# Expert weights of a mixture-of-experts stage: fifteen places for raw slabs and five for their high parts, in place of five and three

## The reference

```python
def grouped_moe(x, w_router, router_bias, w_gate, w_up, w_down):   # 512 tokens, 16 experts in 4 groups of 4
    scores = jax.nn.sigmoid(t @ w_router)
    ...
    g_idx = jnp.argmax(group_score, axis=-1)             # one group of 4 experts for each token
    _, e_local = lax.top_k(in_group, TOP_K)              # 2 of these 4
    ...
    h = silu(einsum('td,edf->tef', t, w_gate)) * einsum('td,edf->tef', t, w_up)   # d 1024, f 256
    y = einsum('tef,efd->td', h * combine[..., None], w_down)
```

## Time and profile before

| | |
|---|---|
| median of 3 runs | 3222.83 us |
| the profiled execution, its own time | 3222.16 us |
| its span, first to last instruction | 3220.1 us |
| granted TensorE clock, mean of the span (1 is 2.4 GHz) | 0.935 |
| PE busy | 2928.7 us (91%) |
| DVE, ACT, POOL busy | 1568.6, 1215.3, 826.5 us |
| slabs of 512 KB: SP, issue to landing, median | 3.7 us (202 transfers) |
| chain that ended last, share of PE | 74% |

### The profile page before, as it was taken

One profiled execution on the slowest core, in us unless ns is written; L12 is line 12 of the kernel. 1 busy time (PEld: TensorE's weight loads), 2 busy tenths in 40 slices (PEclk: granted clock), 3 DMA queues, 4 the chain that ended last, 5 costly groups with the idle time before them and its releaser, 6 DMA issues.

```text
span 3220.1 us, 54157 instructions
## 1 busy us (share of the span) xinstructions
PE 2928.7 (91%) x22694; PEld 2317.3 (72%) x22694; DVE 1568.6 (49%) x2880; ACT 1215.3 (38%) x2134; POOL 826.5 (26%) x814
## 2 busy tenths in 40 slices
PE   7899999999889999999899899998978887898998
PEld 6788888888767878887577677777756655556566
DVE  3544555455424344342443454566667766542433
ACT  2333333333322243232433344543255655442341
POOL 4222222222122100000345243541000055523243
PEclk9899899989889999999899898999999999878999
DMA  3111111111033333332122122224327877411112
GB/s 130 37 32 41 32 41 35 41 31 38 28 111 109 102 99 96 94 97 77 43 65 70 47 69 63 82 66 151 98 81 257 275 248 230 148 38 53 36 56 69
DMA packets 101266, 283.09 MB, mean 88 GB/s; under 512 B 11392, under 2 KB 11392, under 8 KB 99744
## 3 DMA queue, kind: packets, MB, share of 16 engines
q1 hardware_dynamic: 81968, 209.11, 21.5%
q0 software_dynamic: 14592, 60.56, 5.6%
q10 hardware_dynamic: 4464, 9.96, 0.8%
HBM read 261.24 MB, written 18.35 MB: 87 GB/s over the span
## 4 chain that ended last, share of the span: by engine, by line
PE 74%; DVE 10%; ACT 8%; DMA 5%; issue 2%; POOL 1%; ACTq 0%; DVEq 0%; SPq 0%; POOLq 0%
PE psum L478 72%; DVE arena L410 5%; ACT arena L395 4%; DMA ring<-in_w 3%; ACT arena L403 3%; DMA ring<-in_w,arena_whole 2%; PE psum L482 2%; DVE arena L419 2%; DVE ring L410 2%; ACT L390 1%; POOL ring L3488 1%; DVE arena L414 1%; DVE arena L422 1%; DVE arena L434 0%; DMA arena<-in_x 0%
## 5 line engine op out<-in xcount | busy, mean ns | idle before, releaser
L478 PE MATMUL psum<-arena,ring 128*128 128x512 f32 (+3 forms) x6152 | 1442.6, 365 | 13.5 <-DVE arena L410 6.9
L478 PEld LDWEIGHTS psum<-arena,ring 128*128 128x128 f32 (+2 forms) x6152 | 1024.4, 193 | 209.0 <-issue 35.6
L478 PE MATMUL psum<-arena 32*32 32x32 f32 (+16 forms) x12460 | 880.4, 254 | 154.2 <-DVE arena L410 58.4
L478 PE MATMUL psum<-arena,arena 128*128 128x512 f32 (+1 forms) x2896 | 887.4, 391 | 93.3 <-DVE ring L410 68.1
L478 PEld LDWEIGHTS psum<-arena 32*32 32x32 f32 (+10 forms) x12460 | 626.0, 142 | 360.9 <-issue 147.0
L478 PEld LDWEIGHTS psum<-arena,arena 128*128 128x128 f32 x2896 | 525.4, 190 | 257.5 <-DVE ring L410 108.5
L422 POOL CAST ring<-ring 128x512 fp32r<-128x512 f32 x332 | 231.3, 697 | 1370.9 <-DMA ring<-in_w 1248.5
L403 ACT ACTIVATE arena<-psum 128x512 f32<-128x512 f32 (+16 forms) x676 | 290.8, 448 | 746.9 <-PE psum L478 572.5
L410 DVE TENSOR_TENSOR ring<-ring,arena 128x1024 fp32r<-128x1024 f32 (+1 forms) x298 | 352.6, 1183 | 310.5 <-ACT arena L403 305.9
L403 ACT ACTIVATE arena<-ring 128x1024 fp32r<-128x1024 f32 (+1 forms) x298 | 305.6, 1026 | 500.2 <-PE psum L478 334.5
L410 POOL TENSOR_TENSOR ring<-ring,ring 128x512 fp32r<-128x512 f32 x332 | 440.2, 1326 | 26.7
(11 more groups left out here) (50 smaller groups left out, 862.2 us busy)
## 6 DMA issues: line engine op xcount, KB each, us to landing
ring<-in_w SPq DMA_DIRECT2D x202, 512.0 KB, 3.7
ring<-in_w SPq DMA_DIRECT2D x356, 256.0 KB, 2.7
bg<-arena ACTq DMA_DIRECT2D x24, 256.0 KB, 2.3
yd<-arena ACTq DMA_DIRECT2D x7, 512.0 KB, 6.4
arena<-bg POOLq DMA_DIRECT2D x1, 3072.0 KB, 17.0
arena<-in_x SPq DMA_DIRECT2D x1, 2112.0 KB, 15.0
od<-arena POOLq DMA_DIRECT2D x8, 256.0 KB, 2.4
oy<-arena POOLq DMA_DIRECT2D x8, 256.0 KB, 3.0
```

Source lines behind the costliest of these rows:

```text
L478: self.last_ins = self.eng.matmul(out, l, r, start=start, stop=stop, skip_group_check=skip)
```

## The change

During the expert loop, ten more places take raw slabs. Four of them (`soon`) lie in memory that is free once `branches` has ended. Six (`late`) lie where the tokens `x` and two parts of `m.O` are, free once PE has transposed the tokens (event `x_trl`, 1, 3). So slab i of the stage goes to place i modulo 15 of fifteen. Places 0 to 4 of these are the ring's. The high parts get five places in place of three. The room comes from `m.xs` and `m.hot`, which now hold one pair: the selection matrices of the next pair are made in the first expert of blocks 1, 3 and 5, after their last reader, no longer a pair ahead.

```diff
+def slot_of(K, n):
+    first = K.book.now.get(("slab", "slab", "experts", 0))
+    if first is not None and first <= n < first + len(K.m2.we.offs):
+        i = (n - first) % len(K.raw)
+        return (first + i) % RING if i < RING else i
+    return n % RING
+
+def emptied_by(K, slabs):
+    last, out = {}, []
+    for n in range(len(slabs)):
+        out.append(last.get(slot_of(K, n)))
+        last[slot_of(K, n)] = n
+    return out
...
-    m.xt, m.xs, m.hot, m.ysb = M(8 * T), M(16 * T), M(4 * T), [M(1024) for _ in range(2)]
+    m.xt, m.xs, free, m.hot, m.ysb = M(8 * T), M(8 * T), [M(SLAB) for _ in range(5)], M(2 * T), [M(1024) for _ in range(2)]
...
-    wh = [M(1024), M(1024), m.O[:, 10 * T:12 * T]]
+    wh = [M(1024), M(1024), m.O[:, 10 * T:12 * T]] + free[:2]
...
+    m.soon = free[2:] + [M(SLAB)]
+    m.late = [x[:, SLAB * i:SLAB * i + SLAB] for i in range(4)] + [m.O[:, 2 * T:4 * T], m.O[:, 6 * T:8 * T]]
...
     dve_slots(K, m, pos)
     hot(0)
     dve_shares(K, m)
-    hot(1)
     for b in range(BLOCKS):
...
             if e == 0:
                 V.apart().wait_ge(*at("e_rowed", b))
                 V.apart().cp(m.sw[b % 2], out_of(K, 1, 4, "e_rows", b), "e_rows", b)
+                if b % 2 and b // 2 + 1 < PAIRS:
+                    hot(b // 2 + 1)
...
-            if g + 1 < PAIRS:
-                hot(g + 1)
...
-            slot = n % RING
-            G.wait_ge(*at(*K.P.slabs[n - RING][2]))
-            G.ready().indirect_dma_start(K.ring[:, slot * SLAB:slot * SLAB + SLAB], None, by_row,
+            slot = slot_of(K, n)
+            G.wait_ge(*at(*K.P.slabs[before[n]][2]))
+            G.ready().indirect_dma_start(K.raw[slot], None, by_row,
...
-                if n >= RING and off is not None:
-                    sp.wait_ge(*book.at(*slabs[n - RING][2]))
...
+                slot = slot_of(K, n)
+                if before[n] is not None:
+                    sp.wait_ge(*book.at(*slabs[before[n]][2]))
+                elif slot >= RING + len(m2.soon):
+                    sp.wait_ge(*book.at("x_trl", 1, 3))
+                elif slot >= RING:
+                    for e in ("pe", "act", "dve"):
+                        sp.wait_ge(*book.at("end", e, "branches"))
```

More of the change, by code:

```diff
@@ L579, in raw_of @@
     size = run.offs[i][1]
-    return n, K.ring[:, n % RING * SLAB:n % RING * SLAB + size], K.ring_r[n % RING][:, 0:size]
+    return n, K.raw[slot_of(K, n)][:, 0:size], K.ring_r[slot_of(K, n)][:, 0:size]
 def act_hi(K, run, i):
@@ L2095, in memory2 @@
     m.esg = [m.O[:, 8 * T + 256 * i:8 * T + 256 * i + 256] for i in range(4)]
-    wh = [M(1024), M(1024), m.O[:, 10 * T:12 * T]]
+    wh = [M(1024), M(1024), m.O[:, 10 * T:12 * T]] + free[:2]
     m.x_r, m.xh_r = M.rounded(x, T), M.rounded(m.xh, T)
-    m.we = Run(K, "experts", run_of(w0 + 89 * SLAB, 96) + [(None, SLAB)] * 72, wh, [("b_sum", 23)] * 3)
+    m.we = Run(K, "experts", run_of(w0 + 89 * SLAB, 96) + [(None, SLAB)] * 72, wh, [("b_sum", 23)] * 5)
     m.wrh, m.wrl = M.rounded(M(256), 128)
@@ L3175, in rows @@
             for j in range(4):
-                P.mm(bk(o)[:, 0:4], m.hot_r[4 * (b // 2 % 2) + j][:, S], w[:, 4 * j:4 * j + 4], n == 0 and j == 0, n == 1 and j == 3)
+                P.mm(bk(o)[:, 0:4], m.hot_r[j][:, S], w[:, 4 * j:4 * j + 4], n == 0 and j == 0, n == 1 and j == 3)
         P.did("e_rowed", b)
@@ L3181, in weights @@
         P.wait_ge(*at("lo", "experts", i))
-        return m.we.hi[i % 3], K.ring_r[n % RING]
+        return m.we.hi[i % len(m.we.hi)], K.ring_r[slot_of(K, n)]
     def up(b, e):
@@ L3268, in placed @@
             A.wait_ge(*at("e_xsum", g, k))
-            A.copy(m.xs_r[8 * (g % 2) + k][:], out_of(K, 1, T, "e_xs", g, k), "e_xs", g, k)
+            A.copy(m.xs_r[k][:], out_of(K, 1, T, "e_xs", g, k), "e_xs", g, k)
     def turned(b, e):
@@ L3326, in hot @@
         for j in range(4):
-            V.ts(m.hot_r[4 * (g % 2) + j][:], m.slots["number"], pos[:, j:j + 1], -256.0 * g, SUB, EQ, *(("e_hot", g) if j == 3 else ()))
+            V.ts(m.hot_r[j][:], m.slots["number"], pos[:, j:j + 1], -256.0 * g, SUB, EQ, *(("e_hot", g) if j == 3 else ()))
     def gated(b, e):
@@ L3483, in pool_experts @@
     by_row = wall.rearrange("p (s c) -> (p s) c", c=SLAB)
+    before = emptied_by(K, K.P.slabs)
     for n, (off, size, done) in enumerate(K.P.slabs):
         if off is None:
-            slot = n % RING
-            G.wait_ge(*at(*K.P.slabs[n - RING][2]))
-            G.ready().indirect_dma_start(K.ring[:, slot * SLAB:slot * SLAB + SLAB], None, by_row,
+            slot = slot_of(K, n)
+            G.wait_ge(*at(*K.P.slabs[before[n]][2]))
+            G.ready().indirect_dma_start(K.raw[slot], None, by_row,
                                      bass.IndirectOffsetOnAxis(ap=m.place[:, 4 + (done[2] - 96) // 24:5 + (done[2] - 96) // 24], axis=0),
@@ L4169, in layout_engines @@
     half = K.mem.rounded(ring[:, :], HALF)
+    K.raw = [ring[:, n * SLAB:n * SLAB + SLAB] for n in range(RING)]
     K.halves = [half[2 * n:2 * n + 2] for n in range(RING)]
@@ L4190, in layout_engines @@
     m2.floor = m1.floor
+    K.m2 = m2
+    K.raw += m2.soon + m2.late
+    K.ring_r += [K.mem.rounded(q, SLAB)[0] for q in m2.soon + m2.late]
     K.mem.limit += at["con"]["sel16"][0] - early
@@ L4271, in _ @@
             slabs = K.P.slabs
+            before = emptied_by(K, slabs)
             for n, (off, size, done) in enumerate(slabs):
-                if n >= RING and off is not None:
-                    sp.wait_ge(*book.at(*slabs[n - RING][2]))
                 if off is None:
                     continue
-                slot = n % RING
-                eng.dma_start(ring[:, slot * SLAB:slot * SLAB + size], wall[:, off:off + size]).then_inc(*book.up("slot%d" % slot, ("slot%d" % slot, n), by=16))
+                slot = slot_of(K, n)
[6 more added lines that the diff above has]
+                        sp.wait_ge(*book.at("end", e, "branches"))
+                eng.dma_start(K.raw[slot][:, 0:size], wall[:, off:off + size]).then_inc(*book.up("slot%d" % slot, ("slot%d" % slot, n), by=16))
                 if slabs[n][2] == ("slab", "gates", 27):
```

10 lines of the change are left out of this document (5 added, 5 removed).

## The result

The changed kernel takes 3149.72 us (median of 4 runs, 3143.29 to 3159.00) against 3225.18 us before (4 runs beside them, 3220.64 to 3229.49). The ratio is 0.9768, with a 95% interval of 0.9739 to 0.9798: by the ratio 74.8 us less (65 to 84). The forecast was 3140 us, 82.5 less. The profiled execution is the slowest of the four (3159.0 us), so I compare stages inside the traces, not its whole time.

What follows compares the result with a forecast made beforehand. The prediction took the five-place ring as the bound, 1.82 us a slab, with PE next. The loop falls from 356.5 to 268 + 6 = 274 us, 82.5 less: 3222.2 - 82.5 = 3139.7, said as 3140, range 3129 to 3160.

Steps and rivals of the forecast that it cites:

- The ring's turn: Expert loop: load, copy, subtraction and matmuls of one place take 9.1 us for five slabs, 1.82 us a slab.
- 268 + 6 = 274: Expert loop: PE's work sums to 268 us, plus 6 us of waits, for 274 us in place of 356.5.
- The 6 us for waits: Expert loop: added to PE's sum for low parts, DVE at 95% beside PE, and short DMA gaps; ends 1 and 20.
- the last block's debt: Last block of the loop: four more adds stand in DVE's queue (5 us); as the only loss, 1 us.
- the small work of PE: Expert loop: eight transposes and eight narrow matmuls a block, taken at 1.7 us a block, 12 us in all.
- 322 GB/s: Expert loop: DMA rate expected from the stage's own shares; 86.5 MB would take 269 us, ending at 2662, PE at 2663.
- Rival 2: Expert loop: landings get longer with more in flight; at 300 GB/s the whole takes 3153 us; chance 10%.
- Rival 1: Blocks 4 to 6: POOL's gathers set the pace from 1.97 us each; at 2.3 the whole takes 3163 us; chance 8%.
- Rival 3: Expert loop: DMA gives only 241 GB/s, the loop keeps its length, squares cost 3.1 us: whole 3226 us; chance 2%.
- Rival 4: Expert loop: DVE's low parts wait for whole gathers, 68 us more on DVE: whole 3190 us; chance 2%.
- with five it is four slabs, 5.5 us: Expert loop: with five high parts, a low part is asked for four slabs ahead of PE, 5.5 us, against 2.8 with three.
- The layer norm: Ahead of the loop: two more ACT copies delay the squares 3.1 us, covered by DVE's centring: cost 0, uncovered 3.1.

Runs made afterwards that it cites:

- the experiment: Changed kernel with DVE's four additions of the last block moved from its four experts into its last four down slabs: loop 272.3 us, whole 3157.02 us, ratio 0.9776.

## Why the prediction was right

**What bounds.** Right. The ring's turn was the bound: ten more places take away all waits for landings, and with the two high parts the loop is 80.0 us shorter where 82.5 were forecast. Four more places would have done nearly as much (278.6 us).

**The sum of the loop.** Forecast 268 + 6 = 274, measured 276.5. PE's slabs and `placed` are 232.7 + 23.1 = 255.8, and PE's waits 5.9. That leaves 14.8 us for transposes, narrow matmuls and steps between, 2.1 a block where I took 1.7. The 6 us for waits was nearly exact, but where they fall was only half foreseen: 3.5 us are the last block's debt (2.5 of it in two waits), and 2.4 are spread over the experts before. I gave that debt 1 us; the experiment gave back 4.2. So the small work of PE was put 2.8 us too low, and the split of the 6 us was wrong while its sum was right, which is luck.

**The DMA.** My 322 GB/s as the most the stage would get was too low: it ran at 364 to 367 for 40 us at a stretch. The mean over the loop is 304 GB/s, because PE asks for no more. At 365 GB/s the 86.5 MB need 237 us, so PE, with 268, is the bound by 31 us and not by a hair. The bound was rightly named, for a reason that was worse than it is. The landings in the loop did get longer, harmlessly: SP's took 5.3 and 5.5 us in the median (ring and new places), where they took 4.6 in the loop before; the 3.7 in the table of the kernel before is over the whole program. Three signs for the profile after were missed: a DMA share above 0.9 (0.83 over the loop), over 310 GB/s (304), and landings above 6 us, which only 49 of POOL's have (6.3). All three hang on the DMA being nearly the bound, which it was not. Rival 2 is out.

**Rival 1** is out by 25.5 us, and was the right one to watch. **Rival 3** is out with 276.5 us. **Rival 4** is out; the rows are below.

**The halves of the change.** The prediction costed the fifteen places and the five high parts side by side. Places alone give 52.6 us, high parts alone -16.1, both 80.0. My step "with five it is four slabs, 5.5 us" needs a ring that is deep enough beyond the high parts: four slabs more did (nine places), two did not (seven), three was not tried. With ten slabs more the forecast stood, but I had not seen the condition.

**The layer norm.** Cost 0, as forecast: 43.30 us from the last sum of the branches to `placed(0)` before and 43.65 after (43.31 to 43.72 in the other kernels, with and without the two copies).

**The time.** 3149.7 against 3140: the loop accounts for 2.5 us of this. Another 3 us are the base: the forecast starts from 3222.2, and the kernel before took 3225.2 beside the changed one. The last 4 us are within the spread of the unchanged stages. The lower bound from the ratio is 65 us of gain, the upper 84, and both 80.0 and 82.5 lie inside.

## What to carry to other kernels

Look-ahead and buffers belong together: count the slabs between the event that releases a transfer and the one that releases its first reader, times the bound engine's step, and compare with a landing. Beside that, the whole turn of a place divided by the number of places must stay under that step. Where either is too little, deeper second-stage buffers can make things worse, since the copy that asks early stands at the head of its queue and holds what the bound engine needs. And measure a stage from an event at its start to one at its end in each trace: here that repeated to 1 us in two profiles, while whole runs of one kernel spread over up to 29.

## What was unexpected of the hardware

**Gathers fall in step with DVE.** POOL's transfer instructions in the changed kernel, 2541 to 2544.5 us, and DVE's four low parts in that time:

```profile
2541.03 0.94 POOL L3507 DMA_INDIRECT arena<-in_w,arena_whole  x1 [0.30 <-issue]
2542.28 0.94 POOL L3507 DMA_INDIRECT arena<-in_w,arena_whole  x1 [0.30 <-issue]
2543.52 0.96 POOL L3507 DMA_INDIRECT arena<-in_w,arena_whole  x1 [0.30 <-issue]
```

```profile
2538.66 5.01 DVE L410 TENSOR_TENSOR arena<-arena,arena 128x1024 fp32r<-128x1024 f32 x4
```

The low parts end at 2539.91, 2541.16, 2542.42 and 2543.67. A gather starts 0.13 to 0.15 us before such an end and is done about 0.8 behind it; 0.30 later the next one starts, again just before an end. So beside an unbroken row of low parts the pace is 1.25 us, DVE's own. Of the 72 gathers 66 start within a low part, and all of these are done 0.73 to 0.88 us behind its end; one that starts far from that end takes up to 1.94 (1.82 in the earlier trace rows). I had this as a remark against rival 1; in the loop it holds for about half: 38 of the 71 steps are 1.24 to 1.28 us, the others longer, since DVE's row is broken in each expert. Groups by shape, 2406 to 2684 us:

```profile
L410 DVE TENSOR_TENSOR arena<-arena,arena 128x1024 fp32r<-128x1024 f32 x110 | 134.8, 1225 | 15.1 <-ACT arena L403 11.0 <-DVE arena L410 0.2
...
L3507 POOL DMA_INDIRECT arena<-in_w,arena_whole x49 | 57.1, 1166 | 187.1 <-PE psum L478 175.2 <-issue 11.9
```

DVE's low parts take 1225 ns in the mean from 2538 to 2660 us, where the gathers lie, and 1225 to 1226 from 2406 to 2536 us, where there is none. The Trainium skill, "SBUF — State Buffer", section "SBUF: two separate sides", has an exclusive lock that blocks whichever comes second. The trace agrees for POOL behind DVE, and differs for DVE behind POOL.

**With more slabs under way the rate is higher.** With five places the stage moved 242 and 261 GB/s at a share of 0.76 and 0.80, with fifteen 364 to 367 at 0.98, with nine 363 and 352 at 0.98 and 0.95 (2480 to 2520 and 2560 to 2600 us of each). So the rate per share is higher too: 326 and 318 before, 371 to 374 after. Why, these runs do not show.

**The granted clock differs between executions of one kernel** in one and the same piece of work: 0.78 and 0.72 for the kernel before, 122.3 and 128.8 us long (1 is 2.4 GHz; a mean between the levels 1.2 and 2.4). What decides it these runs do not show.
